# Two output sums of a value unit, taken in turns on TensorE instead of one after the other

## What is computed

```python
s1, i1 = lax.top_k(s[:, :, 0], PEER_TOPK)
s2, i2 = lax.top_k(s[:, :, 1], PEER_TOPK)
...
act = jax.nn.gelu(jnp.einsum('td,ted->te', xb, eu[ib]))
return jnp.einsum('te,ted->td', wb * act, ev[ib])
```

## Time and profile before

| | |
|---|---|
| median of three executions | 2361.59 us |
| the profiled execution | 2363.25 us, its span 2361.5 us |
| TensorE matmul busy | 2250.6 us (95%), 16607 matmuls |
| VectorE busy, ScalarE busy | 1379.3 us (58%), 841.7 us (36%) |
| granted TensorE clock, mean of the span | 0.978 |
| first v matmul to last v matmul | 1518.4 to 2343.4 us |

### The profile page before, as it was taken

One profiled execution on the slowest core, in us unless ns is written; L12 is line 12 of the kernel. 1 busy time (PEld: TensorE's weight loads), 2 busy tenths in 40 slices (PEclk: granted clock), 3 DMA queues, 4 the chain that ended last, 5 costly groups with the idle time before them and its releaser, 6 DMA issues.

```text
span 2361.5 us, 38526 instructions
## 1 busy us (share of the span) xinstructions
PE 2250.6 (95%) x16607; PEld 2131.6 (90%) x16607; DVE 1379.3 (58%) x1911; ACT 841.7 (36%) x752; POOL 18.6 (1%) x60
## 2 busy tenths in 40 slices
PE   5797889989999999999999999899999999999997
PEld 1385677878999999999999999899999999999996
DVE  4236565463488886777663334366566566655668
ACT  1121342242334343445543333233333333333331
POOL 0000000000000000000000000000000000000000
PEclk8799999999999999999999999999999999999998
DMA  9976556857545555555555557565555655555542
GB/s 374 388 301 249 214 196 250 317 218 285 197 163 183 187 189 199 188 202 224 211 211 199 184 192 257 206 226 201 207 211 202 230 215 210 200 202 210 206 160 79
DMA packets 118137, 516.02 MB, mean 219 GB/s; under 512 B 8448, under 2 KB 45696, under 8 KB 62848
## 3 DMA queue, kind: packets, MB, share of 16 engines
q1 hardware_dynamic: 71904, 430.35, 49.4%
q10 hardware_dynamic: 45968, 82.17, 9.5%
q0 software_dynamic: 144, 1.73, 0.2%
HBM read 471.92 MB, written 41.99 MB: 218 GB/s over the span
## 4 chain that ended last, share of the span: by engine, by line
PE 89%; DMA 4%; DVE 3%; ACT 2%; issue 1%; ACTq 1%; SPq 0%; DVEq 0%
PE ps L1418 14%; PE ps L1419 14%; PE ps L1424 14%; PE ps L1675 11%; PE ps L1683 11%; PE ps L1676 11%; DMA raw<-in_w_stream_dram 4%; PE ps L1646 3%; PE ps L1456 2%; PE ps L1494 2%; PE ps L1495 2%; PE ps L1501 2%; PE ps L1475 1%; ACT w_hi L1118 1%; PE ps L1623 0%
## 5 line engine op out<-in xcount | busy, mean ns | idle before, releaser
L568 DVE TENSOR_TENSOR w_lo<-raw,w_hi 128x2048 fp32r<-128x2048 f32 x196 | 449.0, 2291 | 489.4 <-ACT w_hi L1118 487.6
L1418 PE MATMUL ps<-act_hi,w_hi 128*128 128x288 f32 x2624 | 716.4, 302 | 16.7 <-ACT w_hi L1118 14.4
L1419 PE MATMUL ps<-act_lo,w_hi 128*128 128x288 f32 x2624 | 708.7, 296 | 0.0
L1675 PE MATMUL ps<-gw_hi,w_hi 128*128 128x288 f32 x2048 | 548.1, 296 | 7.6 <-ACT w_hi L1118 7.6
L1676 PE MATMUL ps<-gw_lo,w_hi 128*128 128x288 f32 x2048 | 547.4, 296 | 0.0
L1418 PEld LDWEIGHTS ps<-act_hi,w_hi 128*128 128x128 f32 x2624 | 496.3, 189 | 39.2 <-issue 36.4
L1118 ACT ACTIVATE w_hi<-raw 128x2048 fp32r<-128x2048 f32 x212 | 405.7, 1914 | 344.5 <-DMA raw<-in_w_stream_dram 245.4
L1419 PEld LDWEIGHTS ps<-act_lo,w_hi 128*128 128x128 f32 x2624 | 495.4, 189 | 0.4 <-issue 0.2
L1675 PEld LDWEIGHTS ps<-gw_hi,w_hi 128*128 128x128 f32 x2048 | 386.9, 189 | 7.8 <-ACT w_hi L1118 7.8
L1676 PEld LDWEIGHTS ps<-gw_lo,w_hi 128*128 128x128 f32 x2048 | 386.2, 189 | 0.0
L1424 PE MATMUL ps<-act_hi,w_lo 128*128 128x288 f32 x2624 | 375.5, 295 | 3.0 <-DVE w_lo L568 3.0
(11 more groups left out here) (189 smaller groups left out, 1404.3 us busy)
## 6 DMA issues: line engine op xcount, KB each, us to landing
raw<-in_w_stream_dram SPq DMA_DIRECT2D x404, 1024.0 KB, 4.9
gelus<-acc ACTq DMA_DIRECT2D x16, 1152.0 KB, 5.8
gates_dense<-mix ACTq DMA_DIRECT2D x18, 1024.0 KB, 4.9
gates_in<-gates_dense ACTq DMA_DIRECT2D x16, 1152.0 KB, 6.7
act_hi<-gelus ACTq DMA_DIRECT2D x15, 1152.0 KB, 11.4
mix<-in_w_stream_dram SPq DMA_DIRECT2D x4, 1024.0 KB, 9.2
x<-in_x_dram ACTq DMA_DIRECT2D x1, 2304.0 KB, 11.8
out_dram<-acc SPq DMA_DIRECT2D x4, 576.0 KB, 2.8
```

The source lines that it names most:

```text
L568: V.tensor_tensor(w_lo[:, s, :], raw_of(u), w_hi[:, s, :].bitcast(F), ALU.subtract).then_inc(lo_ready, 1)
L1418: mm(bank(b, T), w_hi[:, s, w], act_hi[:, c, :], start=c == 0, stop=False)
L1419: n = mm(bank(b, T), w_hi[:, s, w], act_lo[:, c, :], start=False, stop=False)
L1675: mm(bank(2 + b, T), w_hi[:, s, w], gw_hi[:, par, e, :], start=e == 0, stop=False)
```

## The change

Each half's sum used to run whole: 16 high matmuls of half 0, 16 of half 1, 8 low ones of half 0, 8 of half 1. Now both sums are open together, and consecutive matmuls go to the two halves in turn: for each tile e the high activation with the weights of half 0 and of half 1, then the low activation with the same two, and in the low part half 0 and half 1 for each e. Both banks are waited for ahead of the first matmul. The matmuls, their operands and the semaphores raised are the same in number.

```diff
                     pe.wait_ge(hi_ready, unit + (k + 1 + NSPLIT - M0))
+                    halves = [(bank(2 + (2 * k + h) % 4, T), h * P) for h in range(2)]
                     for h in range(2):
-                        b = (2 * k + h) % 4
-                        at_least(pe, vbank_free[b], uses + (2 * k + h) // 4)
-                        for e in range(EG):
-                            w = slice(e * 2 * P + h * P, e * 2 * P + (h + 1) * P)
-                            mm(bank(2 + b, T), w_hi[:, s, w], gw_hi[:, par, e, :], start=e == 0, stop=False)
-                            n = mm(bank(2 + b, T), w_hi[:, s, w], gw_lo[:, par, e, :], start=False, stop=False)
+                        at_least(pe, vbank_free[(2 * k + h) % 4], uses + (2 * k + h) // 4)
+                    for e in range(EG):
+                        for gw in (gw_hi, gw_lo):
+                            for out, o in halves:
+                                w = slice(e * 2 * P + o, e * 2 * P + o + P)
+                                n = mm(out, w_hi[:, s, w], gw[:, par, e, :], start=e == 0 and gw is gw_hi, stop=False)
                     n.then_inc(pe_hi, 1)
                     pe.wait_ge(lo_ready, unit + (k + 1 + NSPLIT - M0))
-                    for h in range(2):
-                        b = (2 * k + h) % 4
-                        for e in range(EG):
-                            w = slice(e * 2 * P + h * P, e * 2 * P + (h + 1) * P)
-                            n = mm(bank(2 + b, T), w_lo[:, s, w], gw_hi[:, par, e, :], start=False, stop=e == EG - 1)
-                        n.then_inc(vhalf_done if h == 0 else pe_unit, 1)
+                    for e in range(EG):
+                        for out, o in halves:
+                            w = slice(e * 2 * P + o, e * 2 * P + o + P)
+                            n = mm(out, w_lo[:, s, w], gw_hi[:, par, e, :], start=False, stop=e == EG - 1)
+                            if e == EG - 1:
+                                n.then_inc(vhalf_done if o == 0 else pe_unit, 1)
```

## The result

The kernel with the change took 2368.45 us (median of 14 executions, 2366.84 to 2371.75). The kernel before, run beside it, took 2362.72 us (median of 14, 2359.51 to 2364.52), about a microsecond above the three executions known at the time of the prediction. The ratio is 1.0026 with a 95% interval of 1.0018 to 1.0034, so the change makes the kernel slower by 4 to 8 us. The prediction was no difference that can be told, 2361.9 us within 2356 to 2368. It is wrong: the time moved, and it lies just outside the range.

A forecast was written before the change was run, and what follows sets the result against it. TensorE was taken as the bound, its v stage set by matmul count times the distance between starts. All terms were zero except +0.3 us at the end, so 2361.59 became 2361.9 us, range 2356 to 2368, no difference given 0.76.

The forecast's parts named there:

- What bounds the stage: v matmul stage: time is the number of matmuls times 132.8 ns between starts; TensorE waits for nothing in the loops.
- Changes of bank: Consecutive v matmuls: all 48 steps of a unit change bank instead of 4; taken as zero cost.
- the four equal runs of eight: High part before: four runs of eight matmuls, two ending with a bank change, all took 1.06 us.
- The first rival: v units: changes of bank pay, 9 ns each, 50.7 us faster, giving 2311.2 us; chance 0.12, in full or part.
- the price of 2298.6 us: All 6144 v matmuls: estimated new time if the whole 10.3 ns excess per matmul were due to adding into one bank.
- Weights and gated tiles: v units: new weights every step, gated tile every second; no difference taken, between 5.6 us less and 6.0 us more.
- The second rival: High part: new weights at every step cost 1.3 ns per matmul, 5.1 us slower; chance 0.09, including tiles read twice.
- The u units' reversed signs: Other loop's units: pairs of equal weights read slower, 133.4 against 133.1 ns, taken as evidence against a cost of new weights.
- The bound towards slower: v units: if every step took 133.8 ns, 6.42 us a unit, the stage would take 6.0 us more.
- Earlier wait, later additions: Unit edges: second bank awaited 16 matmuls earlier, VectorE's additions up to 0.37 us later; all covered, costing nothing.
- the third rival: Unit ends: additions lose their cover and TensorE waits, 0.81 us a unit, 103 us slower, 2465 us; chance 0.03.
- The end: After the last v matmul: the last additions come 0.24 to 0.37 us later, taken as 0.3 us.

The follow-up runs named there:

- e2: Kernel before with its operand order kept, but every matmul writes the other bank than the one ahead of it; 2364.76 us, ratio 1.0007.
- e11: Kernel before with its banks and weight order, but gated tiles in the change's order (product not kept); 2367.51 us, one execution.
- e12: Kernel before with its banks and gated tile order, but weight tiles in the change's order (product not kept); 2362.18 us, one execution.
- e14: Kernel with the change plus 32 unused bytes per partition ahead of `gw_hi`; 2362.13 us, ratio to the kernel before 0.9995.
- e7: Kernel before with the halves taken in turns in the low part alone; 2368.8 us, one execution, unit 6.440 us.
- e9: Kernel before with units 1 to 5 cut to 256, 224, 192, 160, 128 columns; per high matmul 118.7 ns at 256, 111 ns from 224 down.

## Why the prediction was wrong

- *What bounds the stage* was right: matmuls times the distance between starts, with no wait of TensorE in the loops before or after.
- *Changes of bank*, taken as zero from the four equal runs of eight: right, e2 shows it with a change at every step. The first rival falls, and with it the price of 2298.6 us, which supposed that the excess over 122.5 ns goes with adding into one bank. Those 122.5 ns are an estimate for an isolated matmul from the Trainium skill ("TensorE: Matmul & The Clock Gate", "Back-to-back issue gap"), whose section puts no excess down to banks.
- *Weights and gated tiles* is the step that failed. The text took "the middle, no difference" between bounds of 5.6 us less and 6.0 us more, and the term measured 128 x 40 ns = 5.1 us. The choice of the middle had no row behind it: the term was priced from parts that differed in several things at once, and none had the gated tiles in the new order, as the text itself said. What the runs showed in its place is a distance that goes with the order of the gated tiles (e11 6.413 us a unit, e12 6.373). The second rival's 5.1 us agrees with the measured size by accident: it put the cost on new weights in the high part, and e12 shows that the weights' order costs nothing, while the low part, which that rival left at its price, took a third of the loss (13 of 40 ns). Its 1.3 ns were in part rounding: as means, the low part of before is 2.133 us, 133.3 ns a matmul, so the difference to the high part is 0.83 ns, and 0.83 x 4096 = 3.4 us. The u units' reversed signs were rounding as well: a typical one takes 4.266 and 2.134 us, 133.3 and 133.4 ns.
- *The range.* The bound towards slower, 6.0 us, held: the change costs 5.7 us in all, and its mean distance, 6.413 us / 48 = 133.6 ns, is below the 133.8 taken as the slowest, though the low part alone goes to 2.147 us / 16 = 134.2. What carried 2368.45 us past the end at 2368 is the baseline, whose median came out 1.1 us higher than the one the range was built on. So the number outside the range is in part bad luck; the forecast of no difference is wrong without it.
- *Earlier wait, later additions*: right, and the third rival falls, since TensorE waits for nothing in the loops. The additions form a pair, `gw_hi` ends at 1901.84 and `w_hi` starts 0.26 us after the high part's end, as before; e2, whose halves also end together, keeps 6.373 us.
- *The end*: 0.3 us was right. From the last v matmul, 2343.35 us before and 2346.33 us after, to the first L848 it was 0.71 us (L848 at 2344.06) and is 1.00 us.

The sum with the term as measured, 5.1 + 0.3 = 5.4 us, agrees with the difference of the medians, 5.7 us, inside its interval of 4 to 8. Shown: the loss comes from the order in which the gated tiles are read, at the addresses they have (e11, e12, e14), and what one part leaves behind changes the next (e7). Open: why an order and a place give a distance, and what is carried over. That the shift decides the sign is shown for one shift only; others were not tried.

## What to carry to other kernels

When a stage is a gapless stream of equal matmuls, a new sequence of streamed tiles can change the distance between starts, and a nanosecond per matmul is 6.1 us, or 0.26%, here. Read that distance from starts of loop units, where units agree to a nanosecond, and price a new sequence as unknown, with both signs, instead of from the average of the old ones. Alternating output banks or weights was free here, and the loss turned with 32 bytes of placement, so it belongs to the order at its layout, not to the idea of taking the sums in turns.

## What the runs showed of the hardware that was not expected

- The same matmuls at the same addresses ran at 132.5 or 134.2 ns each, depending on the sequence ahead of them (e7 against before), and the mean held through a whole high part, unit after unit.
- 32 bytes of placement moved a unit from 6.373 to 6.380 us in the order of before and from 6.413 to 6.360 in the order of the change.
- With a weight load per matmul, the distance stopped falling at 111 ns: from 224 columns down a narrower gated tile saved nothing (e9).
